# A projection kernel's matmuls, from 512 moving columns to two halves of 256

## What is computed

```python
for l in range(DEPTH):                                   # DEPTH = 2
    x = x + 0.5 * swiglu_ffn(x, ffn1_norm[l], ffn1_w_gate[l], ffn1_w_up[l], ffn1_w_down[l])
    h = rms_norm(x, mix_norm[l])
    aq, ak, av, bq, bk, bv, cq, ck, cv, cg, gates = jnp.split(h @ w_in[l], split_points, axis=-1)
    ...   # three kinds of attention on aq..cg, each with a gate out of `gates`
    x = x + merged.astype(x.dtype) @ w_out[l]
    x = x + 0.5 * swiglu_ffn(x, ffn2_norm[l], ffn2_w_gate[l], ffn2_w_up[l], ffn2_w_down[l])
```

## Time and profile before

| what | value |
|---|---|
| median of the runs | 1642.67 us (1639.84 to 1644.08) |
| the profiled execution, its device time | 1641.94 us |
| its span, first to last instruction | 1640.0 us |
| TensorE matmul busy | 1615.6 us, 99% |
| VectorE busy | 1298.3 us, 79% |
| ScalarE busy | 918.1 us, 56% |
| mean granted clock of TensorE | 0.996 |

### The profile page before, as it was taken

One profiled execution on the slowest core, in us unless ns is written; L12 is line 12 of the kernel. 1 busy time (PEld: TensorE's weight loads), 2 busy tenths in 40 slices (PEclk: granted clock), 3 DMA queues, 4 the chain that ended last, 5 costly groups with the idle time before them and its releaser, 6 DMA issues.

```text
span 1640.0 us, 29782 instructions
## 1 busy us (share of the span) xinstructions
PE 1615.6 (99%) x13092; PEld 1550.3 (95%) x13092; DVE 1298.3 (79%) x1462; ACT 918.1 (56%) x1080; POOL 210.4 (13%) x126
## 2 busy tenths in 40 slices
PE   8999999999999999999999999999999999999997
PEld 8999988999999999999988999999999988899997
DVE  7887888678789888988878678876998598696654
ACT  6554655675464555554656675464555557454543
POOL 1000100000140001200100000031323368300000
PEclk9999999999999999999999999999999999999999
DMA  7667654434566665676754444565555423235551
GB/s 291 229 261 281 242 191 161 155 131 178 206 225 241 257 252 204 255 280 234 279 184 158 151 154 155 182 226 180 194 194 179 154 104 129 78 129 202 185 202 54
DMA packets 47664, 317.56 MB, mean 194 GB/s; under 512 B 5296, under 2 KB 8112, under 8 KB 10032
## 3 DMA queue, kind: packets, MB, share of 16 engines
q1 hardware_dynamic: 47392, 315.64, 52.5%
q10 hardware_dynamic: 144, 0.02, 0.0%
HBM read 314.60 MB, written 1.05 MB: 192 GB/s over the span
## 4 chain that ended last, share of the span: by engine, by line
PE 88%; DVE 8%; ACT 2%; issue 1%; DMA 1%; SPq 0%; POOL 0%; POOLq 0%; DVEq 0%; ACTq 0%
PE ps L1157 25%; PE ps L1159 24%; PE ps L1158 24%; PE ps L1350 3%; PE ps L1352 3%; PE ps L1351 3%; DVE wlo L1796 2%; PE ps L1364 1%; DVE pre L2394 1%; PE ps L1375 1%; DMA raw<-in_w_dram 1%; DVE dA_rows L1796 1%; DVE tmp L1796 1%; DVE qkA L1796 1%; PE ps L1571 0%
## 5 line engine op out<-in xcount | busy, mean ns | idle before, releaser
L1796 DVE TENSOR_TENSOR wlo<-raw,whi 128x2048 fp32r<-128x2048 f32 (+1 forms) x256 | 583.9, 2289 | 96.3 <-ACT whi L654 92.0
L654 ACT ACTIVATE whi<-raw 128x2048 fp32r<-128x2048 f32 (+1 forms) x264 | 500.0, 1905 | 219.0 <-DMA raw<-in_w_dram 218.8
L1157 PE MATMUL ps<-h1hi,whi 128*128 128x256 f32 x1792 | 500.8, 279 | 2.5 <-DVE wlo L1796 2.5
L1159 PE MATMUL ps<-h1lo,whi 128*128 128x256 f32 x1792 | 497.0, 277 | 0.0
L1158 PE MATMUL ps<-h1hi,wlo 128*128 128x256 f32 x1792 | 497.0, 277 | 0.0
L1157 PEld LDWEIGHTS ps<-h1hi,whi 128*128 128x128 f32 x1792 | 337.8, 189 | 6.2 <-DVE h1lo L1847 2.2
L1158 PEld LDWEIGHTS ps<-h1hi,wlo 128*128 128x128 f32 x1792 | 336.9, 188 | 0.0
L1159 PEld LDWEIGHTS ps<-h1lo,whi 128*128 128x128 f32 x1792 | 336.6, 188 | 0.0
L1157 PE MATMUL ps<-hid_hi,whi 128*128 128x256 f32 x880 | 244.5, 278 | 0.3 <-DVE hid_lo L1796 0.3
L1158 PE MATMUL ps<-hid_hi,wlo 128*128 128x256 f32 x880 | 243.7, 277 | 0.0
L1159 PE MATMUL ps<-hid_lo,whi 128*128 128x256 f32 x880 | 243.7, 277 | 0.0
(11 more groups left out here) (360 smaller groups left out, 2540.3 us busy)
## 6 DMA issues: line engine op xcount, KB each, us to landing
raw<-in_w_dram SPq DMA_DIRECT2D x288, 1024.0 KB, 4.8
raw<-in_w_dram SPq DMA_DIRECT2D x8, 256.0 KB, 5.8
c_rows<-in_c_rows_dram SPq DMA_DIRECT2D x2, 1024.0 KB, 9.8
relbias<-in_relbias_dram SPq DMA_DIRECT2D x2, 1024.0 KB, 8.6
pv<-in_pv_dram SPq DMA_DIRECT2D x2, 641.0 KB, 7.4
xT<-in_x_dram SPq DMA_DIRECT2D x4, 256.0 KB, 4.8
raw<-in_w_dram SPq DMA_DIRECT2D x2, 512.0 KB, 6.6
ctxT<-in_ctx_dram SPq DMA_DIRECT2D x1, 1024.0 KB, 6.8
```

The costliest lines, as they stand in the source:

```text
L654: act.activation(whi[:, slot, c], raw[:, slot, c], ACT.Copy).then_inc(hi_done[slot], 1)
L1157: pe.matmul(out, w_hi, hi, start=start, stop=False, skip_group_check=skip)
L1159: return pe.matmul(out, w_hi, lo, start=False, stop=stop, skip_group_check=skip)
L1796: return dve.tensor_tensor(out, a, b, op)
```

## The change

Each product of 512 moving columns becomes two of 256: the columns 0 to 255 of the bank with their three products in a row, then the columns 256 to 511. Each of the 1728 new matmuls loads its stationary operand anew. The flag that starts a bank's accumulation is set only on the first product into the bank; the second half's first product finds its columns cleared by that one.

```diff
                         for tt in range(ST):
-                            out = ps[:, 2 * (g % 2) + tt, :]
                             h_hi, h_lo = (h[:, k, tt * P:(tt + 1) * P] for h in (h1hi, h1lo))
-                            pe.matmul(out, h_hi, w_hi, start=(k == 0), stop=False)
-                            pe.matmul(out, h_hi, w_lo, start=False, stop=False)
-                            ins = pe.matmul(out, h_lo, w_hi, start=False, stop=(k == KT - 1))
+                            for c in (slice(0, S), slice(S, 2 * S)):
+                                out = ps[:, 2 * (g % 2) + tt, c]
+                                first = k == 0 and c.start == 0
+                                pe.matmul(out, h_hi, w_hi[:, c], start=first, stop=False, skip_group_check=True)
+                                pe.matmul(out, h_hi, w_lo[:, c], start=False, stop=False, skip_group_check=True)
+                                ins = pe.matmul(out, h_lo, w_hi[:, c], start=False, stop=(k == KT - 1), skip_group_check=True)
```

## The result

The changed kernel takes 1644.97 us (median of 14 runs), the kernel before 1640.18 (median of 14, the three of the prediction among them). The ratio is 1.0027, 95% interval 1.0016 to 1.0039; applied to 1640.18 us that is 4.4 us, with an interval of 2.6 to 6.4. That is slower beyond the noise, and a little under the bound of 0.3%. The forecast was +1.4 us and 1644.

The account below looks back on a forecast made before the run. TensorE bounds the kernel, busy 1615.6 us of 1640.0. All-short -1.4 us plus 10/18 of 5.1 gives +1.4: 1643.4 from the profiled 1641.94, 1644.1 from the runs' median 1642.67; forecast 1644, range 1639.5 to 1650.

Parts of the forecast that it names:

- the two prices: Start-to-start distance of a 256-column product: 113.3 or 117.8 ns, so a pair saves 2.2 ns or costs 6.8 more.
- The addition of 0.09 us at a row's start: Where a row begins behind transposes, the first distance is 0.09 us longer, with 512 and 256 columns alike.
- the long rhythm: Slower spacing of back-to-back products on TensorE, some 4 to 4.5 ns more per matmul whatever its size, held along a row.
- 10/18: Share of `block3` stretches in the gates' parts at the slower spacing, taken for the split groups: -1.4 + 10/18 x 5.1 us.
- all in the long rhythm except group 0: Case with every split group but the first at 117.8 ns a half: -0.2, +3.6 and +0.3, together +3.7 us.
- The covered part: Groups 2, 3 and half of 4, 120 products a layer, behind VectorE: no gain, 0.16 us overdrawn at the slower spacing.
- (a): Groups all at 113.3 ns a half: -1.4 us, chance 0.17; down to -6.3 us with luck elsewhere, chance 0.05.
- (b): Groups all at 117.8 ns: +3.7 us, within a shared 0.60; with bad luck elsewhere +6.9 us, chance 0.09.
- (c): Holding tokens and moving weights carries a surcharge on each matmul: 122.2 ns a half, +12.1 us, chance 0.09.
- The reading by which the groups pay a fixed 15.5 ns a matmul: 512-column group product as 213.3 ns of columns plus 15.5 fixed per matmul, making a half 122.2 ns.
- The luck in (a) and (b): Shifted timing redraws other rows: 1.5 us for a 40 us stretch's spacing, 1.7 us per stretch at 1.2 GHz, either sign.
- The rule weighed there: Spacing of N / 2.4 + 2.5 ns: two halves 218.3 ns against 215.8 for one product, +1.6 us over 624 products.

Follow-up runs that it names:

- the quarters: The changed kernel with quarters of 128 columns instead of halves of 256, 3456 matmuls: 1824.2 us in one run, 184.9 above the kernel before.

## Why the prediction was right, and where it was not

**Right by its range; the step too small.** 1644.97 lies in the range and 1.0 us from the forecast of 1644, but that closeness is luck. Two errors cancel: the base was taken 2.5 us too high (before had a median of 1642.67 in its first three runs and has 1640.18 now), and the step some 3 us too small. It was forecast at +1.4 us and measured at 4.4 (2.6 to 6.4); the interval lies above it.

**What bounds, and the two prices: right.** TensorE is the bound. 228.8, 113.3 and 117.8 ns are what the groups show after as well, and no third spacing appeared. Group 0 saved 0.11 us a layer, as forecast (0.1). The addition of 0.09 us at a row's start is the same in both widths.

**The step that failed is the frequency of the long rhythm.** I took 10/18 from `block3` rows in a single trace, and weighed it over the rows of the groups as if each drew for itself. The second trace of before and both of after have 14 of 18, and the groups in halves, in both traces of the changed kernel, are long in ten of ten at their start. A better count would not have mended the sum: 14/18 gives -1.4 + 0.78 x 5.1 = +2.6 us. What failed is that rows of halves in the groups draw as `block3` rows do. The sum had a case for what came, "all in the long rhythm except group 0", at +3.7 us.

**The covered part was mis-sized, by 0.2 us a layer.** The traces give 1.57 us a layer where that case says 1.85. Groups 5 to 8 are nearly as forecast (1.24 against 4 x 48 x 6.8 ns = 1.31). Groups 1 to 4 lost 0.44 instead of 0.33 + 0.16 + 0.16 = 0.65: I had left out that behind each of the two waits the next distance was longer too, 0.30 and 0.34 instead of 0.23, which a TensorE that does not wait gets back.

**The rivals.** (a) fell: no row behind other work was short. (b) came in its first half, without the luck or bad luck behind. (c), the surcharge of the swapped roles, fell at once: group 0, with tokens held and weights moving, runs at 113.4 ns. The reading by which the groups pay a fixed 15.5 ns a matmul is wrong with it: two halves cost 226.6 ns and one whole product 228.8.

The luck in (a) and (b) priced a stretch at the lower clock at 1.7 us. One of the two is gone from the trace of after, at full clock with 28 matmuls instead of 18, and nothing is gained by it:

```profile
1324.60:1328.00 3.40, 3.26 (x28) 1.00 0.00 0
1419.50:1422.90 3.40, 3.40 (x19) 0.54 0.00 0
```

The row in that stretch begins 0.83 us later than in before (1325.13 and 1324.30), and the second row behind it 0.86 us later (1337.17 and 1336.31): from 1320 to 1340 us the chain of before runs over VectorE, and TensorE only waits the longer for it.

```profile
by line: DVE pre L2394 45.0%; DVE dA_rows L1796 41.6%; DVE cex L2400 19.5%; issue 10.3%
```

The second stretch does count: in the trace of the other order of the halves, which has none, the row of 168 products around it takes 22.21 us instead of 23.71.

**The rule weighed there.** The Trainium skill, "TensorE: Matmul & The Clock Gate", section on the back-to-back issue gap, gives the spacing of N / 2.4 + 2.5 ns for an isolated product and says that at small widths it leaves out the load of the stationary operand. That rule was right in sign for the kernel as a whole and for another reason than its own. In the short rhythm, the pair of halves was cheaper (group 0: -0.11 us), against it. The Trainium skill, "TensorE: Matmul & The Clock Gate", says in its section on LDWEIGHTS that a load takes the number of its columns over 1.2 ns; for 128 columns an estimate by that page is 106.7 ns. That the quarters came no closer than 111.7 ns on average agrees with it.

**What remains open.** Why a row of halves behind other work begins in the long rhythm, why one settle turns some rows and two turn none, and what the two rhythms are inside the engine. The experiments show that a row of halves holds the rhythm of its start until a longer distance breaks it, and that wide products mostly leave the long one within a few products. Wide products also have room for the load; that this room is the cause was argued, not shown.

## What to carry to other kernels

Matmuls whose columns take no longer than the load of their stationary operand (here 256 columns for a load of 128) had no slack in this kernel: what disturbed the start of a row was paid by every matmul of the row, while wider ones recovered by themselves at most places. Keep the width where it can be had, and count start-to-start distances, not recorded durations. A frequency that stands in a sum should come from more than one trace, and a gain of 3 us that a trace shows can still be lost in what other rows draw.

## What the chip showed that I had not expected

- The same matmuls at the same full clock run at one of two distances, 113.3 or 117.8 ns (228.8 or 233 for 512 columns), for up to hundreds of products, and turn only at a wait or another kind of product, where one distance is longer than the rest (157 ns was enough).
- Eight short matmuls ahead of a row can turn it from one to the other, at 0.34 us for the eight, and eight more can undo that.
- Rows are tied to each other across other work: of the 18 gate rows 10 or 14 were long in all twelve traces, never another number.
- A product of 128 columns costs 111.7 ns where one of 256 costs 113.3.
- A split of 320 and 192 columns costs 261 ns where 256 and 256 cost 227 to 236.
- One execution differs from another of the same program by 2 us in a single feed-forward part, by its rhythm alone (342 or 355 products in 40 us).
